# One kernel, one change: modulation sums with a constant matrix stationary and the 512 sums moving

## The reference

```python
def ada_mods(vec, w, b):
    m = jax.nn.silu(vec) @ w + b
    return [mi[..., None, :] for mi in jnp.split(m, N_MOD, axis=-1)]

def modulate(h, shift, scale):
    return h * (1.0 + scale) + shift
...
        ml = ada_mods(c, ada_w[i], ada_b[i])
...
            mc = ada_mods(c_ctx, ada_w[i], ada_b[i])
...
        x = x + ml[2] * yl
        x = x + ml[5] * sq_relu_mlp(modulate(rms_norm_2(x, norm2_g[i]), ml[3], ml[4]), mlp_w1[i], mlp_w2[i])
```

## Time and profile before

| | us |
|---|---|
| median of three runs | 3950.78 |
| lowest and highest run | 3943.45, 3952.15 |
| span of the profiled execution | 3942.7 |
| TensorE busy in the span | 3801.9 (96%) |
| VectorE busy | 1982.2 (50%) |
| ScalarE, GpSimd busy | 956.5 (24%), 585.3 (15%) |
| mean granted TensorE clock | 0.981 |

### The profile page before, as it was taken

The page is one execution under the profiler, slowest core; times in us unless marked ns, Lnnn a source line. Parts: engine busy times, 40 slices in busy tenths (PEclk is TensorE's granted clock), DMA queues, the critical chain, the costliest instruction groups (busy, mean ns, idle before and its releaser), DMA issues.

```text
span 3942.7 us, 42262 instructions
## 1 busy us (share of the span) xinstructions
PE 3801.9 (96%) x16296; PEld 2605.5 (66%) x16296; DVE 1982.2 (50%) x3455; ACT 956.5 (24%) x2193; POOL 585.3 (15%) x476
## 2 busy tenths in 40 slices
PE   9999999999999999999999899999999999999997
PEld 4458446545655566555554578888568888778886
DVE  2654345635673566555300845654765566244343
ACT  1142214621452212112201632021312111212020
POOL 1001000001000111111200511112432111111111
PEclk8999999999999999999999999999999999999999
DMA  3112331022002123323112414443202444112221
GB/s 130 64 44 87 99 106 56 1 76 86 25 1 63 65 90 124 120 94 128 54 64 76 80 44 150 171 167 101 75 22 86 170 172 150 70 64 86 86 86 43
DMA packets 226949, 342.46 MB, mean 87 GB/s; under 512 B 32256, under 2 KB 100512, under 8 KB 226720
## 3 DMA queue, kind: packets, MB, share of 16 engines
q1 hardware_dynamic: 201552, 321.65, 23.8%
q0 software_dynamic: 6816, 10.01, 1.3%
q10 hardware_dynamic: 18384, 8.11, 0.8%
HBM read 334.08 MB, written 4.06 MB: 86 GB/s over the span
## 4 chain that ended last, share of the span: by engine, by line
PE 90%; DVE 4%; ACT 2%; issue 1%; POOL 1%; DMA 0%; ACTq 0%; DVEq 0%; POOLq 0%
PE psum L1743 44%; PE psum L1493 30%; PE psum L1861 3%; PE psum L1808 3%; PE psum L1838 2%; PE psum L1599 1%; PE psum L1453 1%; DVE small L2735 1%; ACT arena L2192 1%; POOL arena L2916 1%; PE psum L1551 1%; PE psum L1522 1%; PE psum L1534 1%; ACT arena L2180 0%; PE psum L1820 0%
## 5 line engine op out<-in xcount | busy, mean ns | idle before, releaser
L1493 PE MATMUL psum<-HC,ring 128*128 128x256 f32 (+1 forms) x3152 | 1023.7, 484 | 14.2 <-ACT HC L2111 4.5
L1493 PEld LDWEIGHTS psum<-HC,ring 128*128 128x128 f32 x3152 | 599.2, 192 | 430.3 <-issue 371.6
L1743 PE MATMUL psum<-arena,ring 128*128 128x256 f32 (+1 forms) x2304 | 600.4, 416 | 5.2 <-ACT arena L1975 5.2
L1743 PEld LDWEIGHTS psum<-arena,ring 128*128 128x128 f32 x2304 | 435.5, 190 | 147.6 <-ACT arena L1975 10.0
L1743 PE MATMUL psum<-arena 128*128 128x256 f32 (+1 forms) x1792 | 472.3, 417 | 0.4
L1743 PE MATMUL psum<-HC,ring 128*128 128x256 f32 (+1 forms) x1792 | 438.5, 399 | 10.9 <-ACT arena L1975 4.7
L1743 PEld LDWEIGHTS psum<-arena 128*128 128x128 f32 x1792 | 340.4, 190 | 115.4 <-ACT arena L1980 0.7
L1743 PEld LDWEIGHTS psum<-HC,ring 128*128 128x128 f32 x1792 | 341.6, 192 | 86.7 <-issue 10.9
L2873 POOL TENSOR_TENSOR ring<-ring 128x1024 f32<-128x1024 f32 (+1 forms) x80 | 217.4, 2717 | 1220.8 <-DVE arena L2260 1199.4
L2425 DVE SCALAR_TENSOR_TENSOR arena<-ring,cond,arena 128x512 f32<-128x512 f32 x448 | 319.6, 750 | 8.0
L2329 DVE TENSOR_TENSOR arena<-psum,arena 128x384 f32<-128x384 f32 (+2 forms) x80 | 44.5, 556 | 382.6 <-PE psum L1743 382.6
(11 more groups left out here) (229 smaller groups left out, 3907.6 us busy)
## 6 DMA issues: line engine op xcount, KB each, us to landing
ring<-in_mlp_w SPq DMA_DIRECT2D x64, 2048.0 KB, 8.9
ring<-in_ada_w SPq DMA_DIRECT2D x48, 2048.0 KB, 7.9
ring<-in_na_qkv SPq DMA_DIRECT2D x6, 2048.0 KB, 7.9
ring<-in_ab_in SPq DMA_DIRECT2D x5, 2048.0 KB, 8.8
ring<-in_cd_in SPq DMA_DIRECT2D x4, 2048.0 KB, 9.8
ring<-in_pw SPq DMA_DIRECT2D x8, 1024.0 KB, 6.7
ring<-in_at_qkv SPq DMA_DIRECT2D x3, 2048.0 KB, 8.0
ring<-in_ab_out SPq DMA_DIRECT2D x2, 2048.0 KB, 7.7
```

What stands on the lines that cost most here:

```text
L1493: last = nc.tensor.matmul(out, lhs, rhs, start=(k == 0), stop=(k == len(t.pairs) - 1))
L1743: last = nc.tensor.matmul(bank(at, u["T"], u["T"] * m), w[:, i, P * m:P * m + P], x[:, i, :], start=(opens and m == 0 and i == 0), stop=(i ...
```

## The change

The partition sum is turned round: `mean_d` becomes the stationary operand and the 512 sums of one vector are moved through it, one matmul for a vector. Every partition then holds all 512 results, divided by 1024, in a full bank. VectorE multiplies the bank with 1024 and the identity, repeated four times (L2404 of the changed file), in place into `partial`, adds up each of the four stretches of 128 columns (L2409), so that partition p keeps column p of each, and adds the bias (L2411). The bank is free as soon as the first of these has read it (`ada_read`).

The unit of work is now a vector and not a rider: `ride` without a rider takes one pending vector, `ride` with one takes all that are pending, and `flush=True` does the same in the attention output of layer 0, behind which the gains are formed.

```diff
@@ -289,6 +289,7 @@
+        picked = sb("picked", [P, 4])
...
+        ada_read, ada_picked = sem("ada_read"), sem("ada_picked")
@@ -1108,7 +1110,7 @@
-        wide(dram["at_o"], at_out, rides=1, steps=[("gains", 0, [(1, 0), (1, 1)])])
+        wide(dram["at_o"], at_out, rides=1, flush=True, steps=[("gains", 0, [(1, 0), (1, 1)])])
@@ -1436,33 +1438,28 @@
-            def modulation(a):
-
-                layer, j = a[1], a[2]
-                pe.wait_ge(ada_summed, n["ada"] + 1)
+            def modulation(item):
+
+                block_summed, v = item
+                pe.wait_ge(ada_summed, block_summed)
                 open_bank(7)
-                vs = ada_vectors(layer, j)
-                for v in range(vs):
-                    for m in range(4):
-                        last = nc.tensor.matmul(bank(7)[:, 2 * m + v:2 * m + v + 1], partial[:, v, P * m:P * m + P],
-                                                ones[:, :], start=(v == 0 and m == 0), stop=(v == vs - 1 and m == 3),
-                                                skip_group_check=True)
-                last.then_inc(ada_ready, 1)
+                nc.tensor.matmul(bank(7), mean_d[:, :], partial[:, v, :], start=True, stop=True).then_inc(ada_ready, 1)
                 n["ada"] += 1
-                bank_freed[7] = (ada_taken, n["ada"])
-
-            def ride(a):
-
-                if pending:
-                    modulation(pending.pop())
+                bank_freed[7] = (ada_read, n["ada"])
+
+            def ride(a, flush=False):
+
+                for _ in range(len(pending) if a or flush else min(1, len(pending))):
+                    modulation(pending.pop(0))
                 if a:
-                    pending.append(a)
+                    n["riders"] += 1
+                    pending.extend((n["riders"], v) for v in range(ada_vectors(a[1], a[2])))
...
                     if tiles:
-                        ride(a)
+                        ride(a, st.get("flush", False))
@@ -2398,17 +2395,26 @@
-            def ride(a):
-
-                if pending:
-                    layer, j = pending.pop()[1:]
-                    vs = ada_vectors(layer, j)
-                    dve.wait_ge(ada_ready, n["ada"] + 1)
-                    bias = V(f"ada_b{layer}")[:, 4 * j:4 * j + 4].unsqueeze(2).to_broadcast([P, 4, vs])
-                    nc.vector.tensor_tensor(mods[:, layer % 2, 4 * j:4 * j + 4, 0:vs],
-                                            bank(7)[:, 0:8].rearrange("p (m v) -> p m v", v=2)[:, :, 0:vs], bias,
-                                            ALU.add).then_inc(ada_taken, 1)
-                    n["ada"] += 1
+            def pick(item):
+
+
+                layer, j, v = item
+                own = partial[:, v, :].rearrange("p (m f) -> p m f", m=4)
+                dve.wait_ge(ada_ready, n["ada"] + 1)
+                nc.vector.scalar_tensor_tensor(own, bank(7).rearrange("p (m f) -> p m f", m=4), float(D),
+                                               ident[:, :].unsqueeze(1).to_broadcast([P, 4, P]), ALU.mult,
+                                               ALU.mult).then_inc(ada_read, 1)
+                n["ada"] += 1
+                dve.wait_ge(ada_read, n["ada"])
+                nc.vector.tensor_reduce(picked[:, :], own, AX, ALU.add).then_inc(ada_picked, 1)
+                dve.wait_ge(ada_picked, n["ada"])
+                nc.vector.tensor_tensor(mods[:, layer % 2, 4 * j:4 * j + 4, v], picked[:, :],
+                                        V(f"ada_b{layer}")[:, 4 * j:4 * j + 4], ALU.add).then_inc(ada_taken, 1)
+
+            def ride(a, flush=False):
+
+                for _ in range(len(pending) if a or flush else min(1, len(pending))):
+                    pick(pending.pop(0))
                 if a:
                     b, layer, j = a
                     dve.wait_ge(weights_in[b % RING], landed[b])
@@ -2428,7 +2434,7 @@
-                    pending.append(a)
+                    pending.extend((layer, j, v) for v in range(vs))
```

More of the change, by code:

```diff
@@ L1438, in _ @@
             t_base, hid_base = [0], [0]
-            n = dict(block=0, ada=0, norm=0, sq=0, mean=0, spread=0, swap=0, unit=0, pair=0, pas=0, idx=0, down=0,
+            n = dict(block=0, ada=0, riders=0, norm=0, sq=0, mean=0, spread=0, swap=0, unit=0, pair=0, pas=0, idx=0, down=0,
                      yn=0, rope=0, sumsq=0, misc=0, half=0, conv=0)
```

## The result

The changed kernel takes 3953.48 us (median of 14 runs), the kernel before 3944.61 (14 runs beside them): ratio 1.0021, 95% interval 1.0013 to 1.0029, +8.9 us. The profiled spans are 3952.4 and 3942.7, +9.7. The forecast also stood on a median of three runs, 3950.8, that was 6 us above that of fourteen. On the median of fourteen it would read 3969, with a range of 3950 to 3986 that holds the result, so it is the size of the change, +8.9 for +24, that has to be explained and not the place in the range.

What follows compares the result with a forecast made beforehand. It took TensorE, with 90% of the chain, as the bound. Terms of +1.9, +2.4, +1.8, +2.7, +2.3, -1.7 and +14.6 summed to +24.0 us on a median of 3950.8: 3975 us, range 3956 to 3992.

Steps and rivals of the forecast that it cites:

- TensorE's own work: TensorE, all 64 sums: old one-column matmuls worth 53.1 us go, new full-width ones cost 55.0, net +1.9 us.
- The pick: VectorE, per vector: multiply, sum over columns and small add replace one small add, net +1.5 us, bounds 1.2 and 2.3.
- New waits outside the MLPs: TensorE waits at the CD projections' end +2.4, at 951.81 +1.8, attention output's end +2.7, three more places +2.3 us.
- the three places: Behind a rotation's bank, behind the context mean's bank, and a stage end: together +2.3 us, bounds 0 and 4.
- The clock: TensorE's 1.2 GHz stretches behind two-vector riders: two of three spared, perhaps one new, -1.7 us, bounds -5 and +3.
- The loop: MLPs of layers 1 and 2: VectorE's delay passes through in_mlp_w loads to TensorE's weights, +14.6 us, bounds 0 and 30.
- the first rival: The loop has unseen slack (a load landing sooner when issued later, or a shorter pick): 3960 us, chance 0.16.
- The first down unit: Layer 1's MLP, at 2454.59: VectorE's 1.5 us delay reaches the second product through ScalarE's copy, +1.3 us; layer 2, 0.
- The second unit of layer 2: Layer 2's MLP: the next unit's weights come late against a 0.27 us margin, +2.2 us, then +0.2 next round.
- that set's down units: Second set, MLPs of layers 1 and 2: TensorE waits for ScalarE at the second product, +5.1 and +5.5 us.
- part 3: The new waits outside the MLPs: +2.4, +1.8, +2.7 and +2.3 us; new idle mainly between 340 and 1310 would show it too small.
- part 5: The loop through VectorE, in_mlp_w loads and TensorE's weights in the MLPs of layers 1 and 2, +14.6 us.

Runs made afterwards that it cites:

- e8: Kernel before with the new full-width matmul for one-vector riders but the old small add, no pick (modulation values wrong); ratio 1.0003.
- e3: Kernel before with the new sum and pick for the 16 two-vector riders only, old matmuls for one-vector riders; ratio 1.0015.
- e1: The kernel before, unchanged, profiled once more; ratio 1.0004, span 3950.3 us.
- e2: Kernel before with the new sum and pick for the 32 one-vector riders only, old matmuls for two-vector riders; ratio 1.0018.
- e10: Kernel before with 192 one-column matmuls added at the end of TensorE's program; 4017.7 us, added work included.
- e6: Kernel before with two sums over columns put before the old small add of each one-vector rider, without the new matmul; ratio 1.0044.
- e9: Changed kernel with 192 one-column matmuls added at the end of TensorE's program; 4033.2 us, added work included.
- e4: Changed kernel with the sum over columns done three times for each one-vector rider; ratio 1.0078, 3976 us.

## Why the prediction was off, by its steps

1. **TensorE's own work, +1.9: wrong in sign, small.** The new sums cost what was said, 64 x 0.86 = 55.0. The old ones cost more than 0.81: the first product after an old rider took 0.09 longer (3.54 us to the next product against 3.45), which I left out. Then 32 x 0.90 + 16 x 1.79 = 57.4 go, -2.4 in all. e8 shows the sign, -0.4 in each of two layers, and so does the change in the joint MLP, 0.7 us gained from 1345 to 1910. The row was the right one to go by. The page "VectorE: DVE Perf Modes" of the Trainium skill (table under "The TRN2 errata") prices the removed matmuls at max(60, 6 + columns) cycles, which would have made an estimated +42; the trace doesn't agree, at 0.10 us a record for its 0.025.
2. **The pick, +1.5 us a vector: right.** Rows: 0.68, 0.69, 0.08 to the next start; net 1.45 (the rider's sums start 10.12 us after the weight sums, 8.67 before). The rule of the same page of the Trainium skill ("Rules for kernel authors") that a reduce is the slowest operation isn't borne out here: the reduce took 0.69 us, its neighbour 0.68.
3. **New waits outside the MLPs, +9.2: right.** CD end +2.75 (16.13 us from 600.51 to 616.64, before 13.38 from 604.92 to 618.30) for 2.4; at 951.81 +1.8 for 1.8; attention output +2.4 for 2.7; the three places, and a fourth near 898 of 0.25, +2.9 for 2.3. Together 9.9. e3 has them alone. This is the loss that remains: 9.9 us, with 9.7 in all, since the other terms nearly cancel.
4. **The clock, -1.7: right in direction, its size a matter of which executions are compared.** Between 430 and 600 us the low stretches sum to 10.2 us in before, e1, e2, e8 and e10 and to 3.4 in e6, and to 0 in all eight profiles with the new two-vector sums throughout: at half clock 4.5 us given back on average. A part of it is lost again at once: the next stretch, from about 607, lasts 13.7 us in the six of the old kind and 17.1 in six of the eight, so that up to 640 us 3.3 remain. Others come and go with the execution, 3.4 to 20.5 us between 670 and 780 with the old sums and 0 to 20.5 with the new. The first profile of before was poor in them (129.7 us up to 3900, e1 153.6), the change's 133.1, so this pair shows nothing of the gain: the sum of the steps as measured, -2.4 + 9.9 + 1.5, leaves +0.7 for clock and start.
5. **The loop, +14.6: the step that failed. It measured +1.5 in the change, and +8.6 of waits in e9, where the loads of the up units are as long as before's.** So about 7 us of the miss are the length of these loads, and the rest is in the working itself. The pick went into each round as said. But the working kept before's loads (from the end of the sums to the weight sums 8.19 to 9.37 us in the five rounds of layer 1 from 2479.06) in a program where they take 7.42 to 8.69. Four rounds took 24.2 us on average (2488.17 to 2585.13); before they took 23.4, which with the pick would be 24.9, against TensorE's 25.0. So about half of the reserve that I saw gone was still there. In outcome this is the first rival, "a load that lands sooner", to which I gave 0.16; its time, 3960, lies 6.5 above the result, which is the median I stood on. Its reason, that the load is issued later, isn't what e9 shows. Where the up units' loads were as before's, seven tenths of the term are there: e6 costs 8.5 us of waits and 1.8 of clock, e9 8.6 and 1.7.

Three pieces of this term fail with either load. The first down unit, +1.3, costs 0 in the change and 0.1 in e9. VectorE waits for TensorE's product ahead of it anyway, 7.84 us before and 6.29 now; and the load of this unit, 9.2 us from issue to landing before, took 7.8 in the change and 8.1 in e9. Only with e4's pick, twice as dear, did it land late enough to cost 1.5 there. VectorE's wait for the product, in the change:

```profile
2451.46 0.69 DVE L2326 TENSOR_TENSOR arena<-psum,arena 128x512 f32<-128x512 f32 x1 [6.29 <-PE psum L1740]
```

The second unit of layer 2, +2.2 and +0.2, rested on a margin of 0.27 us behind a single long load. It was issued at 3122.12 and landed 10.1 us later, outside the "7.8 to 9.2" that I gave these loads; the same load took 8.1 in the change, where this place costs 0.3, and 7.7 in e9, which has no wait there. Before, and e9:

```profile
3122.12 0.37 SPq L1395 DMA_DIRECT2D ring<-in_mlp_w  x1
```
```profile
3135.53 0.37 SPq L1397 DMA_DIRECT2D ring<-in_mlp_w  x1
...
3143.29 1.23 DVE L2262 TENSOR_TENSOR arena<-ring 128x1024 f32<-128x1024 f32 x1 [7.06 <-DMA ring<-in_mlp_w]
```

These are down units' loads, whose length doesn't go with TensorE's program. The long one is there in four more profiles (9.4 to 9.9 in e1, e2, e8 and e10) and not in the others; why is open.

And the main wait comes earlier than I had it: at the third product of the second up unit of the second set (2596.50 above; 3.15 us in e9), not at that set's down units, where I had put 5.1 and 5.5 and e9 shows 1.2 and 1.5. The weight sums of that unit began at 2585.13, 3.3 us ahead; they hold VectorE's combination of the last products back to 2590.8, ScalarE's hidden tiles behind it, and ScalarE's copy for TensorE behind those:

```profile
2594.68 0.61 ACT L1957 ACTIVATE arena<-arena 128x512 f32<-128x512 f32 x1
2595.33 0.63 ACT L1959 ACTIVATE arena<-arena 128x512 f32<-128x512 f32 x1
2595.87 0.58 ACT L1972 ACTIVATE arena<-psum 128x512 f32<-128x512 f32 x1
```

It is the pattern that the prediction described for the down units, met one place sooner. Three sums of the prediction are also off by 0.1 us (606.6, 5.0 and 5.4 for its 606.7, 5.1 and 5.5), which changes nothing.

Of the signs that were named, TensorE's idle time in front of a down unit's first product is hardly there, and its new idle time lies between 340 and 1310 us. The prediction named that as the sign of a part 3 that was too small; part 3 had its size, and it was part 5 that was too large. VectorE's idle time for in_mlp_w in the two layers didn't get shorter, as was said, but grew from 65.9 us to 86.1.

## What to carry to other kernels

Price an edit on an engine that is not the bound by what stands behind it at each place, vector by vector; the sum of that part came out within 10%. Where a loop runs through a load and has a reserve of about a microsecond, the load's own time is a term of the sum with a range, not a constant taken from one trace: put it in at its shortest and at its longest, and don't rest a margin on one load. And before a difference of 0.2% is explained, profile the same program twice: two executions of the kernel before were 7.6 us apart by the clock alone.

## What was not expected of the hardware

- The loads of in_mlp_w in packets of 2048 bytes end, by their medians, 7.0 to 7.1 us after their issue with 15912 TensorE matmul records in the program, 7.7 to 7.9 with 16104, 8.3 to 8.5 with 16272 to 16680, in four or five kernels each, wherever the records stand; VectorE's 768 more instructions do nothing to them. Loads of the same size in packets of 1024 bytes don't follow (7.8 to 8.2 from issue to landing, by their medians, in all kernels).
- TensorE's low-clock stretches differ between executions of one program: 153.6 and 129.7 us up to 3900 us in two profiles of the kernel before. Three of TensorE's new waits in e4 (2.0 to 4.2 us) had one of 3.4 us behind them; e9's wait of 3.0 us in layer 1 had none.
- 192 one-column matmuls in a row, each with weight loads of its own in the trace, took 82.08 us at the end of e9 and of e10, all at 1.2 GHz. The clock had fallen before them, and it did not rise.
- Behind a rider of one-column matmuls the next product took 0.09 us more than elsewhere; behind the full-width ones it did not.
